# One gate stage, modulation vectors summed over four iterations instead of one block in each

## The chip, the cores and the metric

One core of a Trainium2 chip. The metric is the device time of one launch in microseconds, the median of several runs. The engines are TensorE (PE, with its weight loads as PEld), VectorE (DVE), ScalarE (ACT), GpSimd (POOL) and SyncE (SP), which issues nearly all loads.

## The reference, cut to what matters

A decoder layer on 288 tokens (256 of a prompt, 8 x 4 of samples), width 2048, all float32. The part that the change touches is `mod`, six vectors of 2048 for each of 9 sequences:

```python
mod = (c @ w_ada + b_ada)[:, None, :]                 # c: 9 x 2048, w_ada: 2048 x 12288
sh1, sc1, gt1, sh2, sc2, gt2 = jnp.split(mod, 6, axis=-1)
h = rmsnorm(x, g_norm1) * (1 + sc1) + sh1
proj = h @ w_in
...
branches = jnp.einsum('blnw,nwd->blnd', jnp.stack([y_a, y_b, y_c], axis=2), w_br)
gate = jax.nn.sigmoid(gates.reshape(..., N_BRANCH, D_MODEL))
merged = jnp.sum(gate * branches, axis=2)
x = x + gt1 * (merged @ w_o)
h2 = rmsnorm(x, g_norm2) * (1 + sc2) + sh2
x = x + gt2 * hier_moe(h2, ...)                       # 16 experts, top 2
```

## The kernel before, in words

The kernel runs in stages, one after the other on TensorE: sh1 and sc1 (the first 8 blocks of 512 columns of `w_ada`); the mix stage (48 column tiles of `w_in`); pooling and spatial gating; **the gate stage**; the output projection; routing; and the experts, four groups in a loop.

All projections are computed from split float32: ACT copies half a weight tile (8 x 128 x 128) to `wh`, DVE writes the rest to `wl`, both in rings of three, and TensorE does three matmuls for each k-tile (L1198 to L1200). One half is 24 matmuls with 288 moving columns. `split_hi` waits for `w_used` (TensorE has done the half three before), `half` waits for `lo_ready` (DVE has written the rest).

**The gate stage** is a loop of 16 iterations (`ot`, one column tile of 128 of the width in each) on SyncE, ACT, DVE and TensorE; the last one is written out after the loop on SyncE, ACT and DVE, while TensorE loops over all 16. In one iteration TensorE does, in this order:

- tile 0 of the gates (two halves, bank 0); then chunks 0 and 1 of one block of the modulation,
- tiles 1 and 2 of the gates (banks 1 and 2); then chunks 2 and 3 of that block,
- branches 0 and 1 (one half each); then `ada_select`; then branch 2.

A **block** is 512 columns of `w_ada`, and the 16 blocks of this stage are the four vectors gt1, sh2, sc2 and gt2. In DRAM a block lies as four **chunks** of 1 MB, each with four k-tiles, 8 KB on each partition. `ada_chunk` (L1169) multiplies its four k-tiles at once, each in another group of 32 columns of the array: `cT[:, k]` (128 x 32, 9 sequences and padding) is stationary, 512 columns move, and the four results lie in the four row groups (32 partitions each) of bank 6. They are partial sums of the same block. ACT copies the bank to `part` (L634), and `ada_select` (L1178) sums the four row groups and turns the result to columns on partitions, by four matmuls against `sel` (a matrix with ones at rows 0, 32, 64 and 96 of each sequence). DVE adds the bias and writes four columns of `mod` (L799, which is the line of every `tensor_tensor` of DVE). TensorE's `ada_select` waits for `part_ready` and `mod_ready`.

A float32 matmul shows as two records of each kind in the trace, one of the split kind (float32r) as one.

SyncE issues in each iteration, in this order: chunks 2 and 3 (when chunks 0 and 1 have been used, two buffers `adaw`), the three gate tiles of the next iteration (when DVE has split them), chunks 0 and 1 of the next block (when 2 and 3 have been used), and the branch tile of the next iteration (1.5 MB). All are on one queue.

After the stage ACT and DVE split `merged` to `mh` and `ml`, and x is loaded again; the output projection needs gt1 (`save_x1`), the stage behind it the other vectors. GpSimd waits for the last `ada_sel` before it uses the buffers of `part` and `cT` for sums of squares.

Of the kernel before, what the change touches and what calls it, by code (L numbers as in the profile page):

```python
# [37 lines left out]
NSEQ = 1 + NB  # L38
# [17 lines left out]
SQ_BEFORE = 5  # L56
ADA1_BLOCKS = 8
ADA_CHUNKS = 4
MIX_TILES = 48
MIX_RING = 6  # L60
MIX_IT = MIX_TILES // MIX_RING
# [41 lines left out]
def build(nc, x_in, c_in, conv_in, pool_in, par_in, inv_in, w_ada, w_mix, w_gt, w_br, w_o, pool_w, w_s, b_s,  # L103
          w_r, b_r, w_gate, w_up, w_down, y_out, conv_out, pool_out, v_out):
    ctx = ExitStack()
    with ctx:
# [34 lines left out]
        adaw = [at(f"adaw{k}", (36 + 8 * k) * KB, [P, 4, 512]) for k in range(2)]  # L141
# [37 lines left out]
        wr, mod, par, ident, ones, tri, iota, sel, w4, br, valid, lg, mk, cb, rk, sc, rnd = region(o_p, o_end, *lasting)  # L179
# [4 lines left out]
        cT, part = region(o_q, o_end, ("cT", [P, KT, 32], F32), ("part", [P, 512], F32))  # L184
# [33 lines left out]
        ada_loaded = [sem("ada_loaded0"), sem("ada_loaded1")]  # L218
# [6 lines left out]
        ada_used = sem("ada_used")  # L225
        ada_sel = sem("ada_sel")
# [5 lines left out]
        sq_ready, std_ready, part_ready, hh_ready, hi_ready = (  # L232
            sem(n) for n in ("sq_ready", "std_ready", "part_ready", "hh_ready", "hi_ready"))
# [7 lines left out]
        dch, var_ready, mod_ready, h_ready, hl_ready, lo_ready, rs_ready = (  # L241
            sem(n) for n in ("dch", "var_ready", "mod_ready", "h_ready", "hl_ready", "lo_ready", "rs_ready"))
# [52 lines left out]
        def _(sp):  # L295
# [6 lines left out]
            def ada_src(blk, j):  # L302
                return w_ada[blk, j:j + 1].rearrange("a b p k n -> p (a b k) n")
# [41 lines left out]
                sp.wait_ge(lo_ready, ot * GATE_HALVES + MIX_HALVES)  # L345
                sp.dma_start(brw[:], w_br[ds(ot, 1)].rearrange("a p k c -> p (a k) c")).then_inc(br_loaded, 16)

            def ada_load(ot, j):
                sp.wait_ge(ada_used, ot * 4 + (32 + j - 1))
                sp.dma_start(adaw[j % 2][:], ada_src(ds(ot + ADA1_BLOCKS, 1), j))\  # L350
                    .then_inc(ada_loaded[j % 2], 16)

            for n in range(3):
                gate_load(0, n, 2 * (MIX_TILES - MIX_RING + n) + 2)
            br_load(0)
            sp.wait_ge(mix_mm, WT)
            ada_load(0, 0)
            ada_load(0, 1)
            with sp.Fori(0, KT - 1) as ot:
                ada_load(ot, 2)  # L360
                ada_load(ot, 3)
                for n in range(3):
                    gate_load(ot + 1, n, ot * GATE_HALVES + (MIX_HALVES + 2 * n + 2))
                ada_load(ot + 1, 0)
                ada_load(ot + 1, 1)
                br_load(ot + 1)
            ada_load(KT - 1, 2)
            ada_load(KT - 1, 3)


            def wo_load(v, s):
# [78 lines left out]
        def _(gp):  # L450
            chain = Tally(gp, pch)
# [33 lines left out]
            for f in range(WT):  # L485
# [22 lines left out]
                g, n = f // 2, f // 2 + 1  # L508
# [53 lines left out]

            gp.wait_ge(ada_sel, ADA1_BLOCKS + KT + 1)
            for f in range(KT - 1):
                gp.wait_ge(x1_ready, 3 + f + 1)
                chain.link(gp.tensor_tensor(sqt[:] if f else sqs[:], x1[:, f, :], x1[:, f, :], ALU.mult))  # L568
                if f:
                    last = gp.tensor_tensor(sqs[:], sqs[:], sqt[:], ALU.add)  # L570
# [11 lines left out]
            for k, u in enumerate(BY_GPSIMD):  # L582
                t_, q = UNITS[u]
# [31 lines left out]
        def _(act):  # L615
# [15 lines left out]
            def save_part(n):  # L631
                act.wait_ge(ada_used, n * 4 + 4)
                act.wait_ge(ada_sel, n + 1)
                act.activation(part[:], bank[6][:], ACT.Copy).then_inc(part_ready, 1)  # L634

            def modulate(x, a, shift, q, n):

                act.wait_ge(h_ready, n)
                for f in (4 * q, 4 * q + 2):
                    last = act.activation(x[:, f, 0:TP], x[:, f, 0:TP], ACT.Identity, scale=a[:, f, 0:1],  # L640
                                          bias=mod[:, shift + f, 0:1])
                last.then_inc(hp_ready, 1)
# [55 lines left out]
            def gates_step(ot, unit):  # L698
                for n in range(3):
                    split_hi(unit(ot, 2 * n + 3))  # L700
                    act.wait_ge(w_used, ot * GATE_HALVES + (MIX_HALVES + 2 * n + 2 + NSPL))
                    act.wait_ge(merged_ready, ot + 1)
                    act.activation(sig[:, n, :], bank[n][:, 0:T], ACT.Sigmoid).then_inc(sig_ready, 1)
                    split_hi(unit(ot, 2 * n + 4))
                save_part(ot + ADA1_BLOCKS)
                for k in (9, 10, 11):
                    split_hi(unit(ot, k))

            with act.Fori(0, KT - 1) as ot:
                gates_step(ot, gate_unit)  # L710
            gates_step(KT - 1, gates_then_wo)
            for q in range(3):
                merged_heads(q)
            merged_heads(3)
# [77 lines left out]
        def _(dve):  # L792
            chain = Tally(dve, dch)
# [73 lines left out]
            for s in range(MIX_RING):  # L867
# [10 lines left out]
                if s >= 3:  # L878
                    u = 2 * (s - 3) + 1
# [20 lines left out]
            def gates_step(ot, unit):  # L900
# [12 lines left out]
                split_lo(unit(ot, 11))  # L913
                if unit is gates_then_wo:
                    for q in range(3):
                        merged_rests(q)
                save_mod(ot + ADA1_BLOCKS, ot * 4 + 2 * KT)
                dve.wait_ge(w_used, br0 + 3)
                chain.link(tt(gt[:, 0, :], bank[5][:, 0:T], sig[:, 2, :], ALU.mult))
                tt(dst, dst, gt[:, 0, :], ALU.add).then_inc(merged_ready, 1)  # L920

            with dve.Fori(0, KT - 1) as ot:
                chain.loop(ot, 3)
                gates_step(ot, gate_unit)
            chain.end(KT - 1)
            gates_step(KT - 1, gates_then_wo)
            merged_rests(3)


# [218 lines left out]
        def _(pe):  # L1148
# [16 lines left out]
            def ada_chunk(buf, j, loaded, value):  # L1165

                pe.wait_ge(loaded, value)
                for q in range(4):
                    last = mm(bank[6][32 * q:32 * q + 32, :], cT[:, 4 * j + q, :], buf[:, q, :], start=j == 0,  # L1169
                              stop=j == ADA_CHUNKS - 1, tile_position=(0, 32 * q))  # L1170
                last.then_inc(ada_used, 1)

            def ada_select(n):

                pe.wait_ge(part_ready, n + 1 + 1)
                pe.wait_ge(mod_ready, n + 1)
                for c in range(4):
                    last = mm(bank[7][:, NSEQ * c:NSEQ * c + NSEQ], part[:, P * c:P * c + P], sel[:, 0:NSEQ], start=True, stop=True)  # L1178
                last.then_inc(ada_sel, 1)
# [87 lines left out]
                          (ysp[:, 4 * WT:5 * WT, :], ysp[:, 5 * WT:6 * WT, :])][n]  # L1267
                half(gate_unit(ot, 6 + n), 3 + n, hi, lo, 0, True, True)

            def gates_step(ot):  # L1270
                for n in range(3):
                    pe.wait_ge(sig_ready, ot * 3 + (n + 1))
                    tile(gate_unit, ot, 2 * n, n, hh, hl)
                    if n == 0:
                        pe.wait_ge(part_ready, ot + ADA1_BLOCKS + 1)
                        for j in range(2):
                            ada_chunk(adaw[j], j, ada_loaded[j], ot * 32 + 16)
                for j in range(2, 4):
                    ada_chunk(adaw[j % 2], j, ada_loaded[j % 2], ot * 32 + 32)
                pe.wait_ge(merged_ready, ot + 1)  # L1280
                for n in range(3):
                    branch(ot, n)
                    if n == 1:
                        ada_select(ot + ADA1_BLOCKS)

            pe.wait_ge(yc_ready, WT)
            with pe.Fori(0, KT) as ot:
                gates_step(ot)

            with pe.Fori(0, 5) as v:  # L1290
                for s in range(3):
# [254 lines left out]
```

## Time and profile before

| | |
|---|---|
| median of 3 runs | 1645.53 us (1638.18 to 1647.88) |
| the profiled execution: time, span | 1637.41 us, 1635.7 us |
| mean granted clock of TensorE | 0.972 |
| TensorE busy | 1535.9 us, 94% of the span |
| DVE, ACT, POOL busy | 606.9, 482.1, 238.5 us |
| moved by DMA | 456.47 MB, mean 279 GB/s |

Durations are those of one execution. Idle time of an engine is charged to what ended it; "issue" is time in which the profile shows nothing that the engine waited for. Register, branch and semaphore instructions are not shown as busy. Reads of instructions have queues of their own in the DMA view. The gate stage lies between about 440 and 980 us of the span.

### The profile page before, as it was taken

How to read it: one execution, taken by the hardware profiler on the slowest of the kernel's cores; microseconds unless marked ns; L12 is line 12 of the kernel's file. 1: busy time of each engine (PE TensorE's matmuls, PEld its weight loads, DVE VectorE, ACT ScalarE, POOL GpSimd, SP SyncE). 2: the span in 40 equal slices, each digit the busy share in tenths (PEclk: the TensorE clock that was granted, in tenths of full speed). 3: DMA queues.
4: the chain of work that ended last, by engine and by line, in shares of the span. 5: the costliest groups of instructions: out<-in, count | busy, mean ns of one | idle time of the engine just before them, and what ended most of it. 6: DMA issues, size and time to landing. Idle time of an engine off the chain costs nothing.

```text
span 1635.7 us, 26672 instructions
## 1 busy us (share of the span) xinstructions
PE 1535.9 (94%) x10274; PEld 1184.3 (72%) x10274; DVE 606.9 (37%) x1036; ACT 482.1 (29%) x605; POOL 238.5 (15%) x369
## 2 busy tenths in 40 slices
PE   5779999999999999999999998987999999999994
PEld 2159999999898998989989888975535435444442
DVE  2134444434433343333434345565222222222225
ACT  2123333334234344343443433323101001101102
POOL 0007687800500000000000001222000000000003
PEclk9779999999999999999999999988999999999998
DMA  9994545442276765767567666431899999999992
GB/s 378 422 386 162 183 159 177 165 159 103 91 286 278 283 243 233 294 267 296 219 256 293 267 261 241 176 140 67 345 421 423 421 423 421 422 422 422 422 422 115
DMA packets 63103, 456.47 MB, mean 279 GB/s; under 512 B 7728, under 2 KB 8112, under 8 KB 9440
## 3 DMA queue, kind: packets, MB, share of 16 engines
q1 hardware_dynamic: 62352, 454.66, 69.6%
q0 software_dynamic: 720, 1.41, 0.2%
q8 instruction: 17, 0.28, 0.1%
q14 instruction: 14, 0.11, 0.0%
HBM read 452.93 MB, written 3.12 MB: 279 GB/s over the span
## 4 chain that ended last, share of the span: by engine, by line
PE 84%; DMA 10%; DVE 4%; ACT 1%; issue 1%; SPq 1%; POOL 0%; DVEq 0%; ACTq 0%; PEldq 0%
PE bank L1198 18%; PE bank L1200 17%; PE bank L1199 17%; PE bank L1392 12%; PE bank L1457 6%; DMA ring<-in_w_ada 5%; PE bank L1169 4%; DMA dring<-in_w_down 3%; PE bank L1358 2%; DMA ring<-in_w_up 1%; PE bank L1376 1%; PE bank L1378 1%; PE bank L1178 1%; PE bank L1402 1%; DMA x<-in_x 1%
## 5 line engine op out<-in xcount | busy, mean ns | idle before, releaser
L1198 PE MATMUL bank<-hh,wh 128*128 128x288 f32 x1536 | 458.3, 298 | 8.1 <-DVE wl L799 6.7
L799 DVE TENSOR_TENSOR wl<-mixw,wh 128x1024 fp32r<-128x1024 f32 x224 | 287.9, 1287 | 462.5 <-ACT wh L625 456.0
L1199 PE MATMUL bank<-hl,wh 128*128 128x288 f32 x1536 | 454.4, 296 | 0.0
L1200 PE MATMUL bank<-hh,wl 128*128 128x288 f32 x1536 | 452.8, 295 | 0.0
L625 ACT ACTIVATE wh<-mixw 128x1024 fp32r<-128x1024 f32 x224 | 236.9, 1059 | 346.9 <-PE bank L1200 341.0
L1198 PEld LDWEIGHTS bank<-hh,wh 128*128 128x128 f32 x1536 | 289.2, 188 | 21.8 <-issue 14.9
L1200 PEld LDWEIGHTS bank<-hh,wl 128*128 128x128 f32 x1536 | 290.4, 189 | 0.0
L1199 PEld LDWEIGHTS bank<-hl,wh 128*128 128x128 f32 x1536 | 289.7, 189 | 0.1
L1392 PE MATMUL bank<-ring,xg 128*64 128x512 f32 x512 | 232.3, 598 | 4.5 <-DMA ring<-in_w_up 2.4
L1394 PE MATMUL bank<-ring,xg 128*64 128x512 f32 x512 | 232.6, 598 | 0.0
L1392 PEld LDWEIGHTS bank<-ring,xg 128*64 128x64 f32 x512 | 65.2, 136 | 126.0 <-issue 124.1
L1457 PE MATMUL bank<-dring,hid 128*64 128x512 f32 x512 | 112.5, 594 | 7.0 <-DVE hid L799 3.8
L1198 PE MATMUL bank<-ysp,wh 128*128 128x288 f32 x384 | 116.3, 303 | 0.0
L1199 PE MATMUL bank<-ysp,wh 128*128 128x288 f32 x384 | 113.0, 294 | 0.0
L1200 PE MATMUL bank<-ysp,wl 128*128 128x288 f32 x384 | 112.7, 293 | 0.0
L799 DVE TENSOR_TENSOR wl<-brw,wh 128x1024 fp32r<-128x1024 f32 x48 | 58.8, 1225 | 99.4 <-ACT wh L625 99.4
L1457 PEld LDWEIGHTS bank<-dring,hid 128*64 128x64 f32 x512 | 37.6, 137 | 76.8 <-issue 76.2
L799 DVE TENSOR_TENSOR scaled<-bank,mod 128x32 f32<-128x32 f32 x144 | 20.6, 185 | 173.3 <-PE bank L1358 173.3
L568 POOL TENSOR_TENSOR sqs<-x 128x288 f32<-128x288 f32 x1 | 1.5, 1524 | 557.8 <-DVE x L799 557.8
L1198 PE MATMUL bank<-mh,wh 128*128 128x288 f32 x256 | 76.8, 300 | 6.1 <-DVE ml L799 5.3
L1198 PEld LDWEIGHTS bank<-ysp,wh 128*128 128x128 f32 x384 | 72.0, 188 | 13.4 <-issue 13.4
L606 POOL TENSOR_TENSOR sq<-sq 128x288 f32<-128x288 f32 x8 | 7.0, 871 | 485.3 <-ACT sq L787 485.3
(234 smaller groups left out, 1915.7 us busy)
## 6 DMA issues: line engine op xcount, KB each, us to landing
adaw<-in_w_ada SPq DMA_DIRECT2D x64, 1024.0 KB, 5.9
ring<-in_w_gate SPq DMA_DIRECT2D x64, 1024.0 KB, 16.2
ring<-in_w_up SPq DMA_DIRECT2D x64, 1024.0 KB, 18.2
dring<-in_w_down SPq DMA_DIRECT2D x64, 1024.0 KB, 16.7
mixw<-in_w_mix SPq DMA_DIRECT2D x48, 1024.0 KB, 4.9
mixw<-in_w_gt SPq DMA_DIRECT2D x48, 1024.0 KB, 8.4
ring<-in_w_ada SPq DMA_DIRECT2D x32, 1024.0 KB, 17.9
brw<-in_w_br SPq DMA_DIRECT2D x16, 1536.0 KB, 9.4
```

Of the source, the lines that this page charges most:

```text
L625: act.activation(wh[:, b], src, ACT.Copy).then_inc(hi_ready, 1)
L799: return dve.tensor_tensor(out, a, b, op)
L1169: last = mm(bank[6][32 * q:32 * q + 32, :], cT[:, 4 * j + q, :], buf[:, q, :], start=j == 0, stop=j == ADA_CHUNKS - 1, tile_position=(0, 3 ...
L1178: last = mm(bank[7][:, NSEQ * c:NSEQ * c + NSEQ], part[:, P * c:P * c + P], sel[:, 0:NSEQ], start=True, stop=True)
L1198: mm(out, wh[:, s, k, :], hi[:, first + k, :], start=start and k == 0, stop=False)
L1199: mm(out, wh[:, s, k, :], lo[:, first + k, :], start=False, stop=False)
L1200: last = mm(out, wl[:, s, k, :], hi[:, first + k, :], start=False, stop=stop and k == HALF - 1)
L1358: last = mm(bank[b + h][:, 0:T], y[:, P * (8 * h + j):P * (8 * h + j) + P], sT[before][:], start=part_ == 0, stop=part_ == 1)
L1376: mm(bank[b][:, 256 * d:256 * d + 256], thi[:, t_, f0:f0 + P], oh[:, t_, :], start=t_ == 0, stop=False)
L1392: a = mm(bank[e][0:CAP, :], xg[:, kt, slots], ring8[wg][:, k, :], start=kt == 0, stop=kt == KT - 1, tile_position=(0, 0))
L1394: b = mm(bank[e][CAP:2 * CAP, :], xg[:, kt, slots], ring8[wu][:, k, :], start=kt == 0, stop=kt == KT - 1, tile_position=(0, CAP))
L1457: last = mm(bank[2 + b][CAP * e:CAP * e + CAP, :], hid[e][:, c, :], dring[(16 + 2 * c + e + 3) % 12][:, 512 * b:512 * b + 512], start=c == ...
```

## The change

The blocks of a vector are no longer done one in each iteration. Four blocks, a whole vector, are worked on together through four iterations (`u` 0 to 3 of vector `v`): each matmul of a k-tile goes to the row group of its block, so that bank 6 collects complete sums of four blocks over 16 k-tiles, with the same `cT[:, k]` stationary for all four. A load of 1 MB therefore takes one k-tile of four blocks, 2 KB rows from four places. In the fourth iteration ACT copies the bank once, TensorE turns it (`ada_turn`, four matmuls with 36 columns of `ident` moving), and DVE adds the bias to 16 columns of `mod` at once. The loops over 16 iterations become loops over 4 vectors with four iterations written out in the body; on SyncE, ACT and DVE the last vector is written out behind the loop.

```diff
-            def ada_load(ot, j):
-                sp.wait_ge(ada_used, ot * 4 + (32 + j - 1))
-                sp.dma_start(adaw[j % 2][:], ada_src(ds(ot + ADA1_BLOCKS, 1), j))\
+            def ada_load(v, u, j):
+
+                blocks = ds(v * 4 + ADA1_BLOCKS, 4)
+                sp.wait_ge(ada_used, v * 16 + (4 * u + 32 + j - 1))
+                sp.dma_start(adaw[j % 2][:], w_ada[blocks, u].rearrange("q p k n -> p q k n")[:, :, j, :])\
                     .then_inc(ada_loaded[j % 2], 16)
...
-            with sp.Fori(0, KT - 1) as ot:
-                ada_load(ot, 2)
-                ada_load(ot, 3)
+            def gates_loads(v, u):
+                ada_load(v, u, 2)
+                ada_load(v, u, 3)
+                ot = v * 4 + u
                 for n in range(3):
                     gate_load(ot + 1, n, ot * GATE_HALVES + (MIX_HALVES + 2 * n + 2))
-                ada_load(ot + 1, 0)
-                ada_load(ot + 1, 1)
+                ada_load(v + (u + 1) // 4, (u + 1) % 4, 0)
+                ada_load(v + (u + 1) // 4, (u + 1) % 4, 1)
                 br_load(ot + 1)
...
-            gp.wait_ge(ada_sel, ADA1_BLOCKS + KT + 1)
+            gp.wait_ge(ada_sel, ADA1_BLOCKS + VECTORS + 1)
...
+            def save_vector(v):
+                act.wait_ge(ada_used, v * 16 + (4 * ADA1_BLOCKS + 16))
+                act.wait_ge(ada_sel, v + (ADA1_BLOCKS + 1))
+                act.activation(part[:], bank[6][:], ACT.Copy).then_inc(part_ready, 1)
...
-                save_part(ot + ADA1_BLOCKS)
+                if u == 3:
+                    save_vector(v)
...
+            def save_vector(v):
+
+                dve.wait_ge(ada_sel, v + (ADA1_BLOCKS + 2))
+                first = v * KT + 2 * KT
+                bias = par[:, ds(first, KT)].rearrange("p (q c) -> p q c", q=4).unsqueeze(3).broadcast_to([P, 4, 4, NSEQ])
+                tt(mod[:, ds(first, KT), :].rearrange("p (q c) s -> p q c s", q=4),
+                   bank[7][:, 0:KT * NSEQ].rearrange("p (c q s) -> p q c s", c=4, q=4), bias, ALU.add).then_inc(mod_ready, 1)
...
-                save_mod(ot + ADA1_BLOCKS, ot * 4 + 2 * KT)
+                if u == 3:
+                    save_vector(v)
...
-            with dve.Fori(0, KT - 1) as ot:
-                chain.loop(ot, 3)
-                gates_step(ot, gate_unit)
-            chain.end(KT - 1)
-            gates_step(KT - 1, gates_then_wo)
+            with dve.Fori(0, VECTORS - 1) as v:
+                chain.loop(v, 12)
+                for u in range(4):
+                    gates_step(v, u, gate_unit)
+            chain.end(VECTORS - 1)
+            for u in range(4):
+                gates_step(VECTORS - 1, u, gate_unit if u < 3 else gates_then_wo)
...
-            def gates_step(ot):
+            def ada_rows(buf, k, loaded, value):
+
+                pe.wait_ge(loaded, value)
+                for q in range(4):
+                    last = mm(bank[6][32 * q:32 * q + 32, :], cT[:, k, :], buf[:, q, :], start=k == 0, stop=k == KT - 1,
+                              tile_position=(0, 32 * q))
+                last.then_inc(ada_used, 1)
+
+            def ada_turn(v):
+                pe.wait_ge(part_ready, v + (ADA1_BLOCKS + 2))
+                pe.wait_ge(mod_ready, v + (ADA1_BLOCKS + 1))
+                sequences = ident[:].rearrange("p (q s) -> p q s", q=4)[:, :, 0:NSEQ]
+                for c in range(4):
+                    last = mm(bank[7][:, 4 * NSEQ * c:4 * NSEQ * c + 4 * NSEQ], part[:, P * c:P * c + P], sequences, start=True, stop=True)
+                last.then_inc(ada_sel, 1)
+
+            def gates_step(v, u):
+                ot = v * 4 + u
                 for n in range(3):
                     pe.wait_ge(sig_ready, ot * 3 + (n + 1))
                     tile(gate_unit, ot, 2 * n, n, hh, hl)
                     if n == 0:
-                        pe.wait_ge(part_ready, ot + ADA1_BLOCKS + 1)
+                        if u == 0:
+                            pe.wait_ge(part_ready, v + (ADA1_BLOCKS + 1))
                         for j in range(2):
-                            ada_chunk(adaw[j], j, ada_loaded[j], ot * 32 + 16)
+                            ada_rows(adaw[j], 4 * u + j, ada_loaded[j], ot * 32 + 16)
                 for j in range(2, 4):
-                    ada_chunk(adaw[j % 2], j, ada_loaded[j % 2], ot * 32 + 32)
+                    ada_rows(adaw[j % 2], 4 * u + j, ada_loaded[j % 2], ot * 32 + 32)
                 pe.wait_ge(merged_ready, ot + 1)
                 for n in range(3):
                     branch(ot, n)
-                    if n == 1:
-                        ada_select(ot + ADA1_BLOCKS)
+                    if n == 1 and u == 3:
+                        ada_turn(v)
 
             pe.wait_ge(yc_ready, WT)
-            with pe.Fori(0, KT) as ot:
-                gates_step(ot)
+            with pe.Fori(0, VECTORS) as v:
+                for u in range(4):
+                    gates_step(v, u)
```

## Rows read from the trace of the kernel before

**Rows 1.** The page: busy time of the engines.
```profile
PE 1535.9 (94%) x10274; PEld 1184.3 (72%) x10274; DVE 606.9 (37%) x1036; ACT 482.1 (29%) x605; POOL 238.5 (15%) x369
```
**Rows 2.** Windows of one gate iteration: length, busy (instructions), PEclk, DMA share, GB/s.
```profile
548.77:582.48 33.71, 33.71 (x261) 30.51 (x264) 13.15 (x15) 13.61 (x15) 0.00 (x0) 1.00 0.65 264
919.54:953.25 33.71, 33.71 (x261) 30.50 (x264) 13.15 (x15) 12.32 (x14) 0.00 (x0) 1.00 0.66 264
```
**Rows 3.** The chain of waits in order of time, one gate iteration.
```profile
548.77 1.85 PE bank L1169 x16
563.62 1.85 PE bank L1169 x16
571.99 0.79 PE bank L1178 x8
```
**Rows 4.** Timeline of PE around `ada_select` in that iteration: start, length.
```profile
571.70 0.29 PE L1200 MATMUL bank<-ysp,wl 128*128 128x288 f32 x1
571.83 0.95 PE L1178 MATMUL bank<-sel,part 128*128 128x9 f32 x8
572.64 0.38 PE L1198 MATMUL bank<-ysp,wh 128*128 128x288 f32 x1
572.86 0.30 PE L1199 MATMUL bank<-ysp,wh 128*128 128x288 f32 x1
```
**Rows 5.** Timeline of PE across the jump to the next iteration.
```profile
575.78 0.29 PE L1200 MATMUL bank<-ysp,wl 128*128 128x288 f32 x1
575.92 0.30 PE L1198 MATMUL bank<-hh,wh 128*128 128x288 f32 x1
```
**Rows 6.** Tiles `part` and `mod` (the latter in the gate stage): durations in ns.
```profile
L634 ACT ACTIVATE part<-bank x24: 597/601/601, 25.7 to 970.0; 128x512 f32<-128x512 f32 x24
L799 DVE TENSOR_TENSOR mod<-bank,par x16: 185/188/191, 477.2 to 986.8; 128x36 f32 x15, 128x36 f32<-128x36 f32 x1
```
**Rows 7.** Timeline of DVE behind the last gate iteration.
```profile
982.95 3.89 DVE L799 TENSOR_TENSOR ml<-merged,mh 128x1152 fp32r<-128x1152 f32 x3
986.76 0.19 DVE L799 TENSOR_TENSOR mod<-bank,par 128x36 f32<-128x36 f32 x1
986.87 0.45 DVE L799 TENSOR_TENSOR gt<-bank,sig 128x288 f32<-128x288 f32 x1
996.93 2.36 DVE L799 TENSOR_TENSOR wl<-mixw,wh 128x1024 fp32r<-128x1024 f32 x2 [6.53 <-DMA x<-in_x]
```
**Rows 8.** Tile `adaw`: landing of all its loads; issue and use of one pair.
```profile
DMA to landing us min/median/max: 4.7/5.9/8.1
549.99 1.16 SPq L350 DMA_DIRECT2D adaw<-in_w_ada  x2
563.55 1.49 PE L1169 MATMUL bank<-adaw,cT 128*32 128x512 f32 x12
```
**Rows 9.** DMA view of 8 to 11.3 us: queue, packets, MB, share.
```profile
q1 hardware_dynamic: 550, 0.77, 63.9%
```
**Rows 10.** DMA view of 437:475 (first), 475:979 (next two) and 1261:1605 (last).
```profile
q8 instruction: 3, 0.05, 0.5%
...
DMA packets 17226, 132.86 MB, mean 264 GB/s; under 512 B 1905, under 2 KB 1905, under 8 KB 1905
q1 hardware_dynamic: 17225, 132.85, 65.8%
...
q14 instruction: 1, 0.01, 0.0%
```
**Rows 11.** Window of one pass of the expert loop, as rows 2.
```profile
1261.36:1377.26 115.90, 113.05 (x601) 52.06 (x598) 30.33 (x99) 14.63 (x24) 0.00 (x0) 1.00 1.01 422
```
**Rows 12.** DMA issues (landing last); a wait of PE; a window, as rows 2.
```profile
out_conv_state<-cst POOLq DMA_DIRECT2D x1, 72.0 KB, 1.9
PE bank L1198 <- DVE ml L799: 5.3, 1, 5.3
985.82:989.74 3.92, 3.92 (x16) 3.92 (x17) 2.66 (x5) 1.16 (x1) 0.00 (x0) 0.50 0.33 66
```

More of the change, by code:

```diff
@@ L58 @@
 ADA_CHUNKS = 4
+VECTORS = 4
 MIX_TILES = 48
@@ L356, in _ @@
             sp.wait_ge(mix_mm, WT)
-            ada_load(0, 0)
-            ada_load(0, 1)
-            with sp.Fori(0, KT - 1) as ot:
-                ada_load(ot, 2)
-                ada_load(ot, 3)
+            ada_load(0, 0, 0)
+            ada_load(0, 0, 1)
+            def gates_loads(v, u):
+                ada_load(v, u, 2)
+                ada_load(v, u, 3)
+                ot = v * 4 + u
                 for n in range(3):
                     gate_load(ot + 1, n, ot * GATE_HALVES + (MIX_HALVES + 2 * n + 2))
-                ada_load(ot + 1, 0)
-                ada_load(ot + 1, 1)
+                ada_load(v + (u + 1) // 4, (u + 1) % 4, 0)
+                ada_load(v + (u + 1) // 4, (u + 1) % 4, 1)
                 br_load(ot + 1)
-            ada_load(KT - 1, 2)
-            ada_load(KT - 1, 3)
+            with sp.Fori(0, VECTORS - 1) as v:
+                for u in range(4):
+                    gates_loads(v, u)
+            for u in range(3):
+                gates_loads(VECTORS - 1, u)
+            ada_load(VECTORS - 1, 3, 2)
+            ada_load(VECTORS - 1, 3, 3)
             def wo_load(v, s):
@@ L696, in merged_heads, with gates_step @@
                 act.activation(mh[:, 4 * q:4 * q + 4, :], merged[:, 4 * q:4 * q + 4, :], ACT.Copy).then_inc(mh_ready, 1)
-            def gates_step(ot, unit):
+            def gates_step(v, u, unit):
+                ot = v * 4 + u
                 for n in range(3):
@@ L704, in gates_step @@
                     split_hi(unit(ot, 2 * n + 4))
-                save_part(ot + ADA1_BLOCKS)
+                if u == 3:
+                    save_vector(v)
                 for k in (9, 10, 11):
                     split_hi(unit(ot, k))
-            with act.Fori(0, KT - 1) as ot:
-                gates_step(ot, gate_unit)
-            gates_step(KT - 1, gates_then_wo)
+            with act.Fori(0, VECTORS - 1) as v:
+                for u in range(4):
+                    gates_step(v, u, gate_unit)
+            for u in range(4):
+                gates_step(VECTORS - 1, u, gate_unit if u < 3 else gates_then_wo)
             for q in range(3):
@@ L897, in merged_rests, with gates_step @@
                 tt(ml[:, sl, :], merged[:, sl, :], mh[:, sl, :].bitcast(F32), ALU.subtract).then_inc(ml_ready, 1)
-            def gates_step(ot, unit):
+            def gates_step(v, u, unit):
+                ot = v * 4 + u
                 split_lo(unit(ot, 3))
@@ L920, in gates_step @@
                 tt(dst, dst, gt[:, 0, :], ALU.add).then_inc(merged_ready, 1)
-            with dve.Fori(0, KT - 1) as ot:
-                chain.loop(ot, 3)
-                gates_step(ot, gate_unit)
-            chain.end(KT - 1)
-            gates_step(KT - 1, gates_then_wo)
+            with dve.Fori(0, VECTORS - 1) as v:
+                chain.loop(v, 12)
+                for u in range(4):
+                    gates_step(v, u, gate_unit)
+            chain.end(VECTORS - 1)
+            for u in range(4):
+                gates_step(VECTORS - 1, u, gate_unit if u < 3 else gates_then_wo)
             merged_rests(3)
@@ L1268, in branch @@
                 half(gate_unit(ot, 6 + n), 3 + n, hi, lo, 0, True, True)
-            def gates_step(ot):
+            def ada_rows(buf, k, loaded, value):
[12 more added lines that the diff above has]
+            def gates_step(v, u):
+                ot = v * 4 + u
                 for n in range(3):
@@ L1282, in gates_step @@
                     branch(ot, n)
-                    if n == 1:
-                        ada_select(ot + ADA1_BLOCKS)
+                    if n == 1 and u == 3:
+                        ada_turn(v)
             pe.wait_ge(yc_ready, WT)
-            with pe.Fori(0, KT) as ot:
-                gates_step(ot)
+            with pe.Fori(0, VECTORS) as v:
+                for u in range(4):
+                    gates_step(v, u)
             with pe.Fori(0, 5) as v:
```

## The prediction

> **What bounds the kernel now.** I read the page first, then the windows of single gate iterations, the chain of waits, the timeline of TensorE inside one iteration, and last the DMA view by stretches. The page has TensorE busy for 94% of the span [rows 1], but the share says little by itself; the gate stage, the only one that the change touches, has to be read alone. There one iteration takes 33.71 us, and one near the end of the stage takes the same [rows 2]. TensorE is busy for all of it, DVE and ACT for 13.2 and 13.6 us, DMA for 0.66. The chain of waits runs through the stage on TensorE alone: two blocks of modulation matmuls (1.85 us each) and one summing block (0.79 us) per iteration, between the split matmuls [rows 3]. So 16 iterations make 539 us of the 1635.7, and whatever leaves TensorE there leaves the time, one for one. What leaves ACT or DVE is worth nothing.
>
> **Part 1: twelve of sixteen sums go away.** `ada_select` is 4 float32 matmuls, shown as 8 records. Its price is not the 0.79 us of the chain but what it displaces. The split matmul before it starts at 571.70, the first after it at 572.64 and the second at 572.86 [rows 4]; undisturbed neighbours start 0.133 us apart (24 in 3.2 us; one such step in [rows 5]). So it costs (572.86 - 571.70) - 2 x 0.133 = 0.89 us. 12 x 0.89 = **10.7 us** less on TensorE. The four that stay have 36 moving columns in place of 9. The eight records now take 0.10 us each (0.81 / 8). In the modulation blocks 16 records of 512 columns, four side by side, take 1.85 us [rows 3], so one alone 0.46 at most, and 36 columns in proportion 0.03: less than the 0.10 that a record with 128 x 128 weights needs already. I take 0; the bound is 32 records x 0.03 = 1 us.
>
> **Part 2: the matmuls that stay.** Each 1 MB chunk is still worked off by 4 float32 matmuls into the four row groups of bank 6, with 512 moving columns and 32 stationary ones. Only the choice of weights and of rows differs: one k-tile of `cT` for four blocks, in place of four k-tiles for one block. The blocks stay at 1.85 us [rows 3]: 0. A fallout of equal weights in the four groups isn't shown in either direction; the nearest row is this same one.
>
> **Part 3: copies and bias adds.** ACT loses 12 copies of 0.60 us and DVE 12 adds of 0.19 us [rows 6]; both wait for TensorE anyway. Cover gone, the whole of it would be 9.5 us over the stage. The four adds that stay have 144 elements for 36. The only one near the path is the last: DVE does the three `ml` pieces, then this add, then the gate product that lets SyncE load x, and TensorE's next split waits for that load [rows 7]. An operation of 288 elements takes 0.45 us there, so 144 lie between 0.19 and 0.45: +0.1 to +0.3 us, once. I take +0.1. Mod values for the output projection are complete at the same place as before.
>
> **Part 4: the loads.** SyncE issues as many loads in the same order (two chunks, three gate tiles, two chunks, the branch tile), and the waits keep their values. But the rows are now 2 KB from four blocks instead of 8 KB from one. A load lands after 5.9 us, 8.1 at worst; the pair issued at 549.99 is needed at 563.55, so 13.6 us are there [rows 8]. The price of 2 KB rows is bounded by the start of the kernel, where small rows move: 0.77 MB in 3.3 us at 63.9% of the engines is 365 GB/s at full share [rows 9], against 265 / 0.66 = 401 in the gate stage [rows 2]. That is 10% more, or 6.5 us: hidden, and the DMA share of the stage goes from 0.66 to about 0.69. The loads queued behind (gate and branch tiles) move by under 1 us and have half an iteration. 0.
>
> **Part 5: the loop body.** This is what the change adds unsaid. The loop of TensorE now holds four iterations. One iteration has 9 x 24 + 32 + 8 = 256 matmul records and as many weight loads; the new body has 4 x (216 + 32) + 8 = 1000 of each, 2000 instructions where it was 512, and 3 jumps back where there were 15. The DMA view shows what loops cost now. Instruction reads of 16 KB (0.05 MB in 3 packets) come while the first gate iteration runs; in the 504 us after it 17226 packets are 17225 of data and one other, so none of that kind [rows 10]. Nor does the jump leave a gap: 575.78 and 575.92 [rows 5]. The largest loop of the kernel, the expert group with 601 matmuls and 598 weight loads in its window [rows 11], shows none in its later passes either [rows 10]. So a body of 1200 is kept; nothing here shows one of 2000. Either it is kept too (price 0), or the jump finds its target gone and TensorE stands until 16 KB are read. For that the bounds are these. One such packet takes 0.5% of 16 engines in 38 us by three, or 1.0 us [rows 10], and the quickest landing of the whole page is 1.9 us after its issue [rows 12]; the longest stretch for which TensorE stood before a split matmul in this stretch of the kernel is 5.3 us, and the clock was at 0.50 for the 3.92 us of matmuls after it, 2.0 us more [rows 12]. So 0 to 7.3 us for each of 3 jumps. I take a refetch, since 2000 is 1.7 times what is shown to be kept, at 1.9 + 1.0 + 0.5 for the restart = 3.4 us with the clock up (the 2.85 us of idle in an expert pass left it at 1.00, [rows 11]): **+10.2 us**. The bodies of DVE, ACT and SyncE quadruple too; their iterations have some 35 instructions, and they have a wait for TensorE in every half to hide a pause in. 0.
>
> The Trainium skill bears on this in "Runtime: NRT & Kernel Launch", section "Instruction fetch mechanics": TensorE keeps 128 KiB, 2048 instructions, filled in 16 KiB blocks, and a taken branch whose target is not in the window stalls for a fetch. By it 2000 records and some 60 to 80 register and wait instructions would just not fit, and the jump would stall; the same section also speaks of only two lines of 16 KiB, which the expert group's later passes [rows 10, 11] contradict.
>
> **The sum.** -10.7 + 0.1 + 10.2 = -0.4 us on an execution of 1637.41 us (span 1635.7 and 1.7 around it): 1637.0. The median of the runs, 1645.53, lies 8 us above that execution, so I put the same difference on it: **1645 us**, no change.
>
> **Rivals.** (a) The body is kept. For it: no loop of this kernel has ever read an instruction twice; against it: none was this long. Then -10.7 + 0.1 = -10.6: 1635 us, 0.64% faster. Chance 0.27. (b) The jump stalls longer and lets the clock fall, as after the 5.3 us: 3 x 7.3 - 10.6 = +11.3, or 1657 us. Slower than before from 3.5 us a jump, by over 1% from (16.5 + 10.6) / 3 = 9.0 us. For it: the data queue is full at times, and the read must share it; against it: the reads shown took 1.0 us each with data on the same engines. Chance 0.10. (c) Short rows make the chunk loads late. TensorE would stand before the modulation blocks, at all 16 iterations, by what the landing exceeds 13.6 us; by over 1% in sum from 1.7 us an iteration. It takes a landing 2.3 times as long as now, where rows 9 give 1.1. Chance 0.03: some 1675 us. (d) The change doesn't do what it says, the sum of 0.89 being mere overlap that returns elsewhere: with TensorE at 100% there is no such place, 0.02.
>
> **Numbers.** The forecast has the remaining 0.58. Its own range is a stall of 1.5 to 5.4 us: 1639.5 to 1651. The range to hold 8 in 10 takes in (a) with the scatter of the runs, 1638 to 1648 before, and the lower part of (b): 1630 to 1655. About 1%, 16 us, is what this measurement can tell from no change. Faster by over 1% needs (a) and a lucky scatter: 0.04. Slower by over 1%: the upper end of (b), and (c): 0.06. Within: 0.90.
>
> **What would show it.** Per iteration of the gate stage 32.8 us where there is no summing block and 33.7 where there is: part 1. Modulation blocks of 1.85 us: part 2. Chunk loads of 6 to 7 us to landing, no wait of TensorE for them: part 4. In the instruction queue, 23 packets of 16 KB in the run (17 and six for 1488 more instructions) if the body is kept, 40 to 50 if it is read again in each of three passes; and at the three jumps of TensorE an idle of 3.4 us charged to issue, or none. With gaps at the jumps that hold no instruction reads, or with idle before the chunks, my reasons are wrong even if the time is right.

## The result: 2.15% slower

| | time (median) | profiled execution | span | mean clock |
|---|---|---|---|---|
| before | 1641.86 us (1635.68 to 1647.88) | 1637.41 us | 1635.7 us | 0.972 |
| after | 1676.51 us (1673.21 to 1677.19) | 1676.82 us | 1675.1 us | 0.959 |

The ratio of the times, after over before, is 1.0215, with a 95% interval of 1.0185 to 1.0244. The forecast was 1645 us, the range 1630 to 1655.

### The profile after

The page and its parts on DMA and instruction queues. In queue lines the columns are packets, MB and share of 16 engines; the last line is the chunk loads, with the median time from issue to landing (a landing, from here on).

```profile
PE 1539.9 (92%) x10178; PEld 1183.8 (71%) x10178; DVE 607.5 (36%) x1024; ACT 444.1 (27%) x569; POOL 237.7 (14%) x369
...
q8 instruction: 56, 0.92, 0.2%
...
adaw<-in_w_ada SPq DMA_DIRECT2D x64, 1024.0 KB, 11.8
```

TensorE has 96 records fewer of each kind, the twelve sums, as against [rows 1]. But the queue that reads 16 KB of instructions at a time went from 17 packets (0.28 MB) to 56, and a chunk now lands after 11.8 us, not 5.9 [rows 8].

Windows of iterations without a jump or a summing block, columns as in rows 2:

```profile
470.90:503.71 32.81, 32.81 (x253) 29.61 (x256) 13.05 (x14) 10.44 (x12) 0.00 (x0) 1.00 0.80 259
503.71:536.90 33.19, 33.19 (x253) 29.68 (x256) 13.05 (x14) 10.79 (x14) 0.00 (x0) 1.00 0.83 268
```

The first has exactly what the sum gives back: 33.71 us [rows 2] became 32.81, so 0.90. The DMA share is 0.80 for the same bytes, where it was 0.65.

The first jump, in the timeline of PE:

```profile
583.05 0.29 PE L1232 MATMUL bank<-ysp,wl 128*128 128x288 f32 x1
593.36 0.60 PE L1230 MATMUL bank<-hh,wh 128*128 128x288 f32 x1 [10.01 <-issue]
593.76 0.44 PE L1231 MATMUL bank<-hl,wh 128*128 128x288 f32 x1
```

Before, the same two matmuls started 0.14 us apart [rows 5]. Now TensorE stands for 10.01 us, charged to "issue": the profile shows no engine and no load that it waits for. The DMA view of 583.2 to 593.3 shows three instruction reads in that gap, and that of the whole stage (475 to 1020) 40:

```profile
q1 hardware_dynamic: 268, 1.36, 39.2%
q8 instruction: 3, 0.05, 1.7%
...
q8 instruction: 40, 0.66, 0.5%
```

In the trace these three reads begin at 585.2, 587.4 and 591.0 us and take 0.9 us each: they come one after the other, and TensorE starts 1.5 us after the last. The window behind the jump shows the clock at its lower level, 13 matmuls in 3.14 us instead of 24 in 3.2, and later at 1.00:

```profile
593.36:596.50 3.14, 3.14 (x13) 3.14 (x14) 0.00 (x0) 0.00 (x0) 0.00 (x0) 0.50 0.00 0
596.60:602.50 5.90, 5.90 (x49) 5.01 (x51) 1.23 (x1) 2.04 (x2) 0.00 (x0) 1.00 0.00 0
```

The waits of the stage (445.6 to 1018; total, times, longest), and all landings of chunk loads:

```profile
PE bank L1230 <- issue: 27.6, 3, 10.0
PEld bank L1306 <- DMA adaw<-in_w_ada: 17.1, 12, 2.6
PE bank L1306 <- DMA adaw<-in_w_ada: 8.1, 8, 1.7
...
DMA to landing us min/median/max: 7.4/11.8/15.4
```

Three jumps stand for 27.6 us. Some chunk loads come later than the 13.6 us that rows 8 leave them, which costs TensorE 8.1 us of visible idle at eight blocks. The chain shows it as "DMA":

```profile
585.71 7.65 issue
...
603.48 15.38 DMA adaw<-in_w_ada
618.90 1.07 PE bank L1306 x8
```

**The account of the stage** in the two profiled executions: 541.1 us before (439.5 to 980.6), 573.5 after (445.6 to 1019.1), so +32.4. The terms: -10.7 for the sums; +27.6 at the jumps; +5.1 for the half speed behind them (3.1, 3.9 and 3.2 us of work at 0.50, half of it lost); +8.1 for the idle before late chunks, and some 2 more for iterations that are longer than 32.81 us without such idle (33.19 in the second window above). That makes 30 to 32. The other 7 us of the 39.4 between the spans lie ahead of the stage or are scatter; the last section tells what 6 of them are.

### The profile page after: what moved, and what is told of

Read it like the earlier page. It is cut to its first block, busy times and chain, and to the rows that moved or that the text cites. A ratio compares the mean times of both kernels' runs of the same rounds, so it can differ in the third digit from the quotient of the medians.

```text
span 1675.1 us, 26096 instructions
## 1 busy us (share of the span) xinstructions
PE 1539.9 (92%) x10178; PEld 1183.8 (71%) x10178; DVE 607.5 (36%) x1024; ACT 444.1 (27%) x569; POOL 237.7 (14%) x369
## 4 chain that ended last, share of the span: by engine, by line
PE 75%; DMA 18%; DVE 3%; issue 2%; ACT 1%; SPq 1%; POOL 0%; DVEq 0%; ACTq 0%; PEldq 0%
PE bank L1230 16%; PE bank L1232 15%; PE bank L1231 15%; PE bank L1443 10%; DMA adaw<-in_w_ada 7%; PE bank L1508 5%; DMA ring<-in_w_ada 5%; PE bank L1306 3%; DMA dring<-in_w_down 3%; DMA ring<-in_w_up 2%; PE bank L1409 2%; PE bank L1427 1%; PE bank L1429 1%; PE bank L1453 1%; DMA x<-in_x 1%
## 5 line engine op out<-in xcount | busy, mean ns | idle before, releaser
L1230 PE MATMUL bank<-hh,wh 128*128 128x288 f32 x1536 | 461.7, 301 | 35.7 <-issue 27.6
L1231 PE MATMUL bank<-ml,wh 128*128 128x288 f32 x256 | 76.7, 300 | 0.0
## 6 DMA issues: line engine op xcount, KB each, us to landing
adaw<-in_w_ada SPq DMA_DIRECT2D x64, 1024.0 KB, 11.8
```

The lines of the kernel that those rows point to most:

```text
L1230: mm(out, wh[:, s, k, :], hi[:, first + k, :], start=start and k == 0, stop=False)
L1231: mm(out, wh[:, s, k, :], lo[:, first + k, :], start=False, stop=False)
```

## The experiments

Two suspects stand beside one gain, so each got a kernel in which it is alone, one in which it is taken out, and one with both. Ratios are against runs of the kernel before on the same chip.

| kernel | TensorE's loop body | chunk rows | sums | ratio (95%) |
|---|---|---|---|---|
| after | 4 iterations | short, far | 4 | 1.0215 (1.0185 to 1.0244) |
| e1_rows | 4 | 8 KB | 4 | 1.0092 (1.0062 to 1.0123) |
| e4_straight | no loop | short, far | 4 | 0.9945 (0.9924 to 0.9965) |
| e5_both | no loop | 8 KB | 4 | **0.9894 (0.9863 to 0.9924)** |
| e2_short | 1 | short, far | 16 | 1.0052 (1.0035 to 1.0069) |
| e3_unroll4 | 4 | 8 KB | 16 | 1.0135 (1.0105 to 1.0166) |
| e11_unroll4_short | 4 | short, far | 16 | 1.0281 (1.0246 to 1.0315) |
| e12_straight_old | no loop | 8 KB | 16 | 1.0011 (0.9990 to 1.0032) |

### The body alone, and the rows alone

**e3_unroll4**: the kernel before with

```diff
-            with pe.Fori(0, KT) as ot:
-                gates_step(ot)
+            with pe.Fori(0, 4) as v:
+                for u in range(4):
+                    gates_step(v * 4 + u)
```

> The kernel before with one edit: TensorE's loop holds four iterations in its body, 4 times in place of 16. All sums, copies and loads are as before. If the size of the body is what costs: three idles of 8 to 10 us, about 40 reads of 16 KB in the gate stage in place of 3, and 30 to 35 us more (1672 to 1677). If the jump were long for another reason (the new order of waits, or late work of another engine), nothing changes here.

Measured 1659.5 us, +1.35% or 22 us. Its page and waits:

```profile
q8 instruction: 56, 0.92, 0.2%
...
PE bank L1198 <- issue: 14.3, 3, 5.0
```

The body's size alone brings the same 56 packets and three idles, with nothing else changed. But they are 5 us each, not the 8 to 10 that I expected from the changed kernel, and the time is 12.5 us under the lower end that I had set. A jump costs 22 / 3 = 7.4 us with the low clock behind it; the trace has 7.0 (4.8 of idle, and half of the 13.6 us of work that the three low stretches hold).

**e2_short**: the kernel before with SyncE's part of the changed kernel and its address pattern; the host lays `w_ada` out inversely, so that each load fetches the old chunk in 2 KB rows.

```diff
-                sp.dma_start(adaw[j % 2][:], ada_src(ds(ot + ADA1_BLOCKS, 1), j))\
+                sp.dma_start(adaw[j % 2][:], w_ada[blocks, u].rearrange("q p k n -> p q k n")[:, :, j, :])\
...
+        a[8:] = a[8:].reshape(4, 4, 4, P, 4, 512).transpose(0, 4, 1, 3, 2, 5).reshape(16, 4, P, 4, 512)
```

> The kernel before with its loop of one iteration on TensorE, but its chunks laid out in DRAM so that each is read as 512 rows of 2 KB from four places 4 MB apart, by the loads of the changed kernel. If short rows from four places alone make chunks late: landings of 11 to 12 us instead of 5.9, idle before about one modulation block in two or three, together 8 to 14 us: 1650 to 1656. If the lateness came from the jumps: landings near 6.5 us and no change.

Measured 1647.98 us, +0.52%, 2 us under what I expected. Landings and waits:

```profile
DMA to landing us min/median/max: 7.4/11.0/15.0
...
PEld bank L1180 <- DMA adaw<-in_w_ada: 15.7, 12, 3.7
PE bank L1180 <- DMA adaw<-in_w_ada: 7.0, 8, 2.7
```

So the rows alone nearly double the landing, with 17 packets of instructions and no long jump in the run: the jumps don't cause the late chunks. Nor does SyncE's longer loop body, which e9_runs below has as well and at no cost.

### Each taken out of the change

**e1_rows**: the changed kernel with 8 KB rows.

```diff
-                sp.dma_start(adaw[j % 2][:], w_ada[blocks, u].rearrange("q p k n -> p q k n")[:, :, j, :])\
+                sp.dma_start(adaw[j % 2][:], ada_src(ds(v * 4 + (ADA1_BLOCKS + u), 1), j))\
...
+        a[8:] = a[8:].reshape(4, 4, 4, P, 4, 512).transpose(0, 2, 4, 3, 1, 5).reshape(16, 4, P, 4, 512)
```

> The changed kernel with w_ada laid out for it in DRAM, so that each 1 MB chunk is read in 8 KB rows as before the change; four iterations stay written out. If the loss has two parts, long jumps (3 x about 9.4 us idle and 5 us of low clock) and late chunks (about 11 us), this one loses only the first: chunk loads land in 5.9 us, no wait for them, three idles of 8 to 10 us at the jumps stay, and the time is 33 - 11 = 22 us over before (1664). If the jumps cause the late chunks too, the landings stay near 11.8 us and the time near the changed kernel's.

```profile
DMA to landing us min/median/max: 4.7/5.8/8.3
...
PE bank L1229 <- issue: 19.4, 3, 6.7
```

1655.83 us: the landings are those of before, no wait for a chunk is left, and the time falls by 20.7 us, twice what I had given the rows. A part of it is the jumps: 19.4 us in place of 27.6, with the very same TensorE program. They are still longer than the 14.3 us of e3_unroll4, which has the same rows and another body: what sets the length of a jump beside the rows stays open.

**e4_straight**: the changed kernel with TensorE's loop written out.

```diff
-            with pe.Fori(0, VECTORS) as v:
+            for v in range(VECTORS):
                 for u in range(4):
                     gates_step(v, u)
```

> The changed kernel with TensorE's 16 iterations written out without a loop: no jump back is left, while the same number of instruction blocks (about 33) is read in order. If the jump to a block that is gone costs, its 33 us go, and what stays is the late chunks (+11) less the sums (-10.7): 1640 to 1646. If reading the code as such costs, there are as many reads as in the changed kernel and the time stays near 1676.

1630.35 us, 46 us less than the changed kernel and 9 less than before. Reading code is not what costs: its profile has 46 instruction packets, nearly as many as the 56, and no idle charged to issue before a split matmul in the stage. What costs is the jump to a block that is gone. The late chunks are still there (10.7 us to landing), but TensorE idles only 1.5 us for them, and I had them too dear at 11. They cost more than that idle: the next kernel, which differs by the rows alone, is 4.3 us faster. Why they cost less here than in e2_short, which has no long jump either, is not shown.

**e5_both**: the edits of e1_rows and e4_straight together.

> The changed kernel with both costs taken out: chunks in 8 KB rows by the layout in DRAM, and TensorE's 16 iterations written out without a loop. If the change is worth the twelve sums (10.7 us) and nothing else hides, 1628 to 1629 beside 1639 for the kernel before, chunk loads at 5.9 us, no idle before a chunk. It should beat the version with long rows left out (1630.4) by the 1 to 5 us that the late chunks still cost there. If that one was already at the end of the gain, the two are the same.

1626.06 us, 0.9894: the fastest of all. One iteration and the landings, from an execution that took 1637.24 us because the clock fell ahead of the stage (last section); the other four took 1625.5 to 1626.2:

```profile
502.60:535.40 32.80, 32.80 (x250) 29.59 (x250) 13.05 (x14) 10.44 (x12) 0.00 (x0) 1.00 0.68 274
...
DMA to landing us min/median/max: 4.6/5.6/7.0
```

**e12_straight_old**: the kernel before with TensorE's 16 iterations written out.

```diff
-            with pe.Fori(0, KT) as ot:
+            for ot in range(KT):
                 gates_step(ot)
```

> The kernel before with TensorE's 16 iterations written out, nothing else. If reading 33 blocks of code in order is free: the time of before within 0.2%, no idle in the stage. Then the whole 1.06% of the version with both costs taken out is the twelve sums. If straight code is itself faster, part of that gain is not the change's.

Same time as before (1.0011, 0.9990 to 1.0032), with 47 instruction packets. Straight code costs or gains no more than 0.3%, so e5_both's gain is that of the sums in the main: 13 us by the medians, 12 to 22 by the interval of the ratio, 10.7 by the timeline. The interval does not quite take in the 10.7, because the kernel before runs at two levels (last section): the four quick runs of e5_both lie some 12 us under its lower level.

### The two costs together

**e11_unroll4_short**: e2_short and e3_unroll4 in one.

> The kernel before with both costs of the change and without its gain: four iterations in the body of TensorE's loop, and chunks in 2 KB rows from four places in steps of 8 KB. If the two costs merely add (1.35% and 0.52%): 1670. If instruction reads are slower beside such rows, so that the jumps grow from 5 to 9 or 10 us: about 1680 to 1685, with idles of 8 to 10 us at the jumps.

```profile
PE bank L1209 <- issue: 27.3, 3, 9.5
...
PE bank L1180 <- DMA adaw<-in_w_ada: 9.3, 10, 3.0
```

1684.43 us, +2.81%. The two alone make 1.87% (31 us); together 46. The three jumps stand for 27.3 us beside short rows and 14.3 beside long ones [e3_unroll4]. So the reads of instructions suffer from the rows, as the changed kernel and e1_rows (27.6 and 19.4 us) show too, which differ by the rows alone. The DMA view of the first gap of e3_unroll4, 574.9 to 580 us, shows what is missing there:

```profile
q1 hardware_dynamic: 3, 0.02, 1.1%
q8 instruction: 1, 0.02, 1.1%
```

With long rows nearly all data has landed before the jump, and the reads have the DMA engines almost to themselves (in e1_rows too, with 1 data packet from 581.4 to 588.1 us); with short rows 268 data packets move in the gap beside the three reads. That they meet is shown. Whether the number, the slowness or the bytes of those packets delay the reads is not.

### Where a body becomes too long

Kernel before, with three iterations in the body (e7_unroll3; e8_pad with six more summing blocks in each) or two (e13_two; e14_two_pad9 with nine more, e15_two_pad13 with thirteen). The instructions between two jumps are counted in the traces, with register and branch instructions.

```diff
+            with pe.Fori(0, 5) as v:          # e7_unroll3; e13_two: Fori(0, 8), range(2)
+                for u in range(3):
+                    gates_step(v * 3 + u)
+            gates_step(KT - 1)
...
+                for _ in range(6 if more else 0):     # e8_pad: 6; e14_two_pad9: 9; e15_two_pad13: 13
+                    for c in range(4):
+                        last = mm(bank[7][:, NSEQ * c:NSEQ * c + NSEQ], part[:, P * c:P * c + P], sel[:, 0:NSEQ], start=True, stop=True)
```

> The kernel before with three iterations in the body of TensorE's loop (5 times, and the last written out): some 1600 instructions. If the loop is kept up to somewhere near 2000 instructions: no idle at the four jumps, 25 or fewer packets of instructions in the run, and no change in time. If any body of over 1200 is read again: four idles of 5 us and lower clock after them, 20 to 30 us more (about 1665).

> The kernel before with three iterations in the body and the summing block of each repeated six more times, which makes some 1880 instructions in the body (1067 in two iterations, 2123 in four). One look: does the profile show instruction reads in the later passes and an idle at the jumps? If the room is 2048 instructions and all of it holds the loop: no. If one block of it is always taken by reading ahead, so that 1792 are left: yes, at four jumps, of 4.5 to 5.5 us each. The added matmuls themselves cost about 16 x 4.9 = 78 us.

> The kernel before with two iterations in the body of TensorE's loop, 8 times: 1067 instructions, under the 1260 of the expert loop that were kept, and over one iteration's 533. If only the size of the body counts: no idle at the seven jumps, 17 packets of instructions, the time of before within 0.3%.

> As the last, with the summing block repeated nine more times in each iteration: 1355 instructions in the body. One look at the instruction reads and the jumps. Kept: some 19 packets in the run and no idle at the seven jumps. Read again: 50 packets or more and seven idles of 3 to 7 us. The room lies between 1260 and 1593; by blocks of 256, six blocks (1536) would still hold it. The added matmuls cost some 16 x 7.3 = 117 us in both cases.

> The same with thirteen repeats: 1483 instructions. If the room is six blocks wherever the body begins in a block, it needs six or seven of them and is read again if it needs seven; 20 packets and no idle at the jumps if it is kept, some 60 packets and seven idles if not. The added matmuls cost some 16 x 10.5 = 168 us.

| body | instructions | instruction packets in the run | at the jumps | time |
|---|---|---|---|---|
| before | 533 | 17 | nothing | medians of 1638 to 1642 us |
| e13_two | 1063 | 19 | nothing | 1.0010 (0.9991 to 1.0029) |
| e14_two_pad9 | 1351 | 20 | nothing | 1879.5 us |
| e15_two_pad13 | 1479 | 21 | nothing | 1990.06 us |
| e7_unroll3 | 1593 | 59 | 4 idles, 23.5 us | 1.0151 (1.0120 to 1.0183) |
| e8_pad | 1881 | 65 | 4 idles, 12.4 us (three charged to DVE) | 1814.7 us |
| after | 2069 | 56 | 3 idles, 27.6 us | 1.0215 |
| e3_unroll4 | 2123 | 56 | 3 idles, 14.3 us | 1.0135 |

First the page of e15_two_pad13, then that of e7_unroll3 with its waits:

```profile
q8 instruction: 21, 0.34, 0.1%
```
```profile
q8 instruction: 59, 0.97, 0.2%
...
PE bank L1198 <- issue: 23.5, 4, 6.3
```

Up to 1479 instructions a body is kept, from 1593 it is read again in every pass. Blocks of 256 instructions are how "Runtime: NRT & Kernel Launch", section "Instruction fetch mechanics", of the Trainium skill counts them; six of them are 1536, which fits, but two points don't prove it. Of the two outcomes set out for e7_unroll3 the second came, with 25 us more by the ratio and 29 by the medians. But its condition, any body of over 1200, is too wide: those of e14_two_pad9 and e15_two_pad13 are kept. How long a jump stands does not follow the length of the body: 3.1 us of idle at 1881 instructions, 4.8 at 2123, 5.9 at 1593. The padded kernels took far more than their expected times, since their clock fell as well (last section); only their reads and jumps are used.

### What it is in the rows

Three more layouts, each read in 512 rows of 2 KB by the kernel before; the host lays `w_ada` out so that each load still fetches the old chunk:

```diff
+                rows = w_ada[ds(ot + ADA1_BLOCKS, 1), j].rearrange("a p k n -> (a p k) n")           # e6_adjacent
+                sp.dma_start(adaw[j % 2][:], rows.rearrange("(q p) n -> p q n", p=P))\
...
+                runs = w_ada[blocks, u].rearrange("q p k n -> q (p k) n").rearrange("q (j p) n -> j p q n", p=P)   # e9_runs
+                sp.dma_start(adaw[j % 2][:], runs[j])\
...
+                rows = w_ada[ds(ot + ADA1_BLOCKS, 1)].rearrange("a q p k n -> p k (a q) n")           # e10_pitch
+                sp.dma_start(adaw[j % 2][:], rows[:, j])\
```

> The kernel before with each chunk again read as 512 rows of 2 KB, but all within one contiguous 1 MB of DRAM (k-tile by k-tile), not from four places 4 MB apart. If the row size makes the loads slow (more and shorter packets, whatever their place): landings of 10 to 12 us as with the four places, and 1645 to 1650. If the four places in DRAM do it: landings near 6.5 us and the time of the kernel before.

> The kernel before, its chunks read as 512 rows of 2 KB from four places 4 MB apart, but with the rows of neighbouring partitions next to each other, so that each place is a run of 256 KB (in the changed kernel they lie 8 KB apart). If the four distant places make the loads slow: landings near 11 us and 7 to 9 us more. If it is the step of 8 KB between rows: landings of 6.5 us, as with the one contiguous 1 MB, and no change.

> The counterpart: rows of 2 KB in steps of 8 KB, as in the changed kernel, but all four places within one 4 MB block, 1 MB apart. If the step of 8 KB is the cause: landings near 11 us and 1646 to 1649. If the distance of 4 MB is: 6.5 us and no change.

| kernel | step from partition to partition | four places apart | landing min/median/max | ratio (95%) |
|---|---|---|---|---|
| e6_adjacent | 2 KB | 256 KB | 5.1/6.5/9.1 us | 1.0000 (0.9976 to 1.0024) |
| e9_runs | 2 KB | 4 MB | 5.2/6.4/8.9 us | 1.0014 (0.9991 to 1.0037) |
| e10_pitch | 8 KB | 1 MB | 5.1/6.2/8.7 us | 1.0017 (0.9995 to 1.0038) |
| e2_short | 8 KB | 4 MB | 7.4/11.0/15.0 us | 1.0052 (1.0035 to 1.0069) |

The answer is neither of the two that I had set against each other. Rows of 2 KB land in 6.2 to 6.5 us, the 6.5 that the prediction worked out; neither the step nor the distance alone makes them slow, only both together. In the traces a 2 KB packet takes 127 ns on average in e2_short and 92 to 94 in the other three. Why the two together do this stays open; no other steps or distances were run.

## Why the prediction was wrong, step by step

**Part 1, the sums, was right.** 32.81 us per iteration without one, as forecast (32.8), 33.71 before. Turning 36 columns costs nothing that shows: it displaces the split matmuls by as much as a sum did (578.97 to 580.13, 1.16 us, as 571.70 to 572.86 in [rows 4]). e5_both has the gain in full once nothing is in its way.

**Part 2 was right** (1.85 us a block). **Part 3 was right**: the bias add of 144 elements behind the last iteration took 0.30 us, between the bounds:

```profile
1025.34 0.30 DVE L819 TENSOR_TENSOR mod<-bank,par 128x144 f32<-128x144 f32 x1
```

**Part 4, the loads, failed.** "6.5 us: hidden" was read off small packets at the start of the kernel, 1.4 KB on average [rows 9], of whose places in DRAM the row says nothing. It holds for the size of the rows (e6_adjacent, e9_runs and e10_pitch, whose DMA shares over the stage, 0.68 to 0.70, are the 0.69 forecast) and not for their places (e2_short: 11.0 us, share 0.81). The row was the nearest in size and said nothing of what mattered, the address pattern: I had written "from four blocks" and given that no price and no reason. Rival (c), with 0.03, happened in part: landings of up to 15.4 us against the 13.6 there were. It cost 8 to 9 us alone (e2_short, 0.52%), some 0.5 us an iteration where the rival asks for 1.7.

**Part 5, the loop body, had the mechanism and missed the size.** The reads (40 to 50 packets forecast, 56 found) and the idle at three jumps charged to issue are as it said. The term of 3.4 us a jump failed: it was 1.9 for a landing, 1.0 for a packet and 0.5, one read with the clock up. Alone a jump costs 7.4 us (e3_unroll4): 4.8 of idle and the clock at 0.50 behind it, which I had put in rival (b). Beside short rows it is 9.2 of idle and 1.7 of clock, 10.9 in all. The bound of 7.3 came from one wait for another engine; here several reads came one after the other. Rival (b), with 0.10, was nearest, and its reason, that the read must share the engines with data, fits the gaps of the changed kernel; its 7.3 us was too small as well. And the limit was not where I looked: 1593 instructions are too many already.

The figure of 2048 instructions in "Runtime: NRT & Kernel Launch", section "Instruction fetch mechanics", of the Trainium skill is too high for a body that is to be kept here, by at least 455. Its rule for a taken branch whose target is not in the window, a stall for a fetch, agrees with the runs: reads in the gap at each of the three jumps.

**The sum.** I treated the costs as separate, rival against rival. They happen together and feed each other: 22 + 8.5 alone, 46 together (e11), less 10.7 for the sums makes the 35 measured. The range took in each rival and not their sum, and ended at 1655.

## What to carry to other kernels

Writing iterations out in a loop is only free while the body stays short on TensorE: count its instructions, weight loads included (here bodies up to 1479 were kept, and in the unpadded kernels with 1593 and more each jump cost 7 to 11 us by the traces), and compare the instruction packets of the page before and after. The bodies of SyncE, ACT and DVE, four times as long, cost nothing that shows in e5_both. If TensorE's body must be longer, write the whole loop out; 47 packets in straight code cost nothing beyond 0.3%. And a load with the same bytes and other addresses is another load: lay the array out in DRAM for the order in which it is read, which turned this change from +2.15% to -1.06% together with the straight code.

## Unexpected in the runs

- **The kernel before runs at two levels, 1635 to 1640 us and 1643 to 1648 us, and the kernels near its time scatter in the same way.** What differs shows in the windows ahead of the gate stage. These are 432 to 440 us of before, then of after:

```profile
432.00:440.00 8.00, 6.61 (x42) 5.54 (x43) 6.91 (x22) 0.00 (x0) 7.04 (x13) 1.00 0.11 19
```
```profile
432.00:440.00 8.00, 8.00 (x32) 6.65 (x30) 4.84 (x15) 0.00 (x0) 4.86 (x8) 0.54 0.00 0
```

In the small matmuls of spatial gating the granted clock stays at 1.00 or falls to 0.50 for about 17 us. TensorE has 15.7 us of work in them; half of it is the 8 us between the levels. Profiled executions with the fall took 1646.03 (e9_runs), 1645.10 (e10_pitch) and 1647.52 us (e13_two); those without 1637.41 (before), 1639.17 (e6_adjacent) and 1639.70 us (e12_straight_old). Those of e2_short (1654.51) and e5_both (1637.24) had it too, and are the slowest of their five runs. The changed kernel's profile has the fall, that of before has not, and its gate stage began 6 us later: that is nearly all the rest of the 39.4. What lets the clock fall in one execution and not in the next is not shown.

- **A busy TensorE can lose its clock.** With thirteen more summing blocks in each iteration it was busy for all of the 200 us of the first window of e15_two_pad13 (columns as in rows 2), with a granted clock of 0.84. The second lies in one run of summing blocks (590.2 to 610.0 us):

```profile
560.00:760.00 200.00, 200.00 (x1348) 187.18 (x1346) 52.60 (x60) 54.41 (x60) 0.00 (x0) 0.84 0.45 178
594.60:610.00 15.40, 15.40 (x74) 15.40 (x74) 0.00 (x0) 0.00 (x0) 0.00 (x0) 0.50 0.00 0
```

The clock fell 4.4 us into these matmuls of 9 columns and rose 5 us after the split matmuls had begun again, and so in every iteration: 20 to 24 us at 0.50 in each. The kernel took 350 us more than before where 168 were expected; half of 16 such stretches, some 170 us, is nearly all of the difference.
